# Token sums of the norms over 128 columns, running sums first, and high passes first in the two units behind them

## The reference

```python
def rms_norm(x, g):
    y = xf * lax.rsqrt(jnp.mean(xf * xf, axis=-1, keepdims=True) + RMS_EPS)
    return (y * g.astype(jnp.float32)).astype(x.dtype)
...
def layer_norm(x, g, b):
    mu = jnp.mean(xf, axis=-1, keepdims=True)
    var = jnp.mean(jnp.square(xf - mu), axis=-1, keepdims=True)
    y = (xf - mu) * lax.rsqrt(var + LN_EPS)
    return (y * g.astype(jnp.float32) + b.astype(jnp.float32)).astype(x.dtype)
...
    x = layer_norm(ALPHA * x + mix, ln1_g, ln1_b)
    up = causal_dwconv_2(jnp.einsum('bsd,df->bsf', x, w_up), ffn_conv_w)
    ffn = jnp.einsum('bsf,fd->bsd', jax.nn.silu(a) * b, w_down)
    return layer_norm(ALPHA * x + ffn, ln2_g, ln2_b)
```

## Time and profile before

| | us |
|---|---|
| median of 3 runs | 1235.99 |
| lowest and highest | 1234.67, 1236.5 |
| the profiled execution | 1236.2 |
| its span, first to last instruction | 1234.4 |
| PE busy | 1208.5 (98%) |
| DVE busy | 844.7 (68%) |
| ACT busy | 705.9 (57%) |
| POOL busy | 399.6 (32%) |
| mean granted clock of PE | 0.992 |

### The profile page before, as it was taken

How to read it: one execution, slowest core, us unless ns; L and a number is a source line. 1 busy time by engine, 2 the same in 40 slices (tenths; PEclk the granted TensorE clock), 3 DMA queues, 4 the chain that set the end, 5 groups by cost and what they waited for, 6 DMA issues and landing times. The chain is left out here.

```text
span 1234.4 us, 27264 instructions
## 1 busy us (share of the span) xinstructions
PE 1208.5 (98%) x10242; PEld 1183.6 (96%) x10242; DVE 844.7 (68%) x1458; ACT 705.9 (57%) x1228; POOL 399.6 (32%) x376
## 2 busy tenths in 40 slices
PE   8999999999999999999999999999999999999997
PEld 8998989999999999999999999999999999999997
DVE  5867664676777765767677777755766677777655
ACT  4666566545666654466455666644466555666642
POOL 2006214023334402210338434314610339343313
PEclk8999999999999999999999999999999999999999
DMA  6554445665566666454653666565554654566662
GB/s 242 187 166 142 137 133 153 194 191 169 172 188 197 189 192 189 154 158 151 188 174 123 186 187 198 173 205 155 154 171 142 187 180 128 186 190 187 199 190 87
DMA packets 60288, 212.70 MB, mean 172 GB/s; under 512 B 6688, under 2 KB 7968, under 8 KB 60064
## 3 DMA queue, kind: packets, MB, share of 16 engines
q1 hardware_dynamic: 60192, 211.39, 55.8%
HBM read 210.31 MB, written 1.05 MB: 171 GB/s over the span
## 5 line engine op out<-in xcount | busy, mean ns | idle before, releaser
L1391 DVE TENSOR_TENSOR wlo<-raw,whi 128x1024 fp32r<-128x1024 f32 (+1 forms) x400 | 489.5, 1225 | 302.0 <-ACT whi L733 300.0
L1065 PE MATMUL bank<-shifted,whi 128*128 128x256 f32 x2296 | 639.3, 278 | 1.3 <-POOL shifted L667 1.1
L1066 PE MATMUL bank<-shifted,whi 128*128 128x256 f32 x2296 | 636.2, 277 | 0.0
L1067 PE MATMUL bank<-shifted,wlo 128*128 128x256 f32 x2296 | 635.9, 277 | 0.0
L733 ACT ACTIVATE whi<-raw 128x1024 fp32r<-128x1024 f32 (+1 forms) x400 | 415.7, 1040 | 146.7 <-PE bank L1067 134.4
L1065 PEld LDWEIGHTS bank<-shifted,whi 128*128 128x128 f32 x2296 | 431.5, 188 | 3.1 <-POOL shifted L667 1.3
L1067 PEld LDWEIGHTS bank<-shifted,wlo 128*128 128x128 f32 x2296 | 431.7, 188 | 0.0
L1066 PEld LDWEIGHTS bank<-shifted,whi 128*128 128x128 f32 x2296 | 431.1, 188 | 0.0
L634 POOL TENSOR_TENSOR fprod<-ugate,uval 128x256 f32<-128x256 f32 x66 | 99.4, 1506 | 210.1 <-DVE uval L1736 204.5
L1065 PE MATMUL bank<-fhi,whi 128*128 128x256 f32 x528 | 146.1, 277 | 0.0
L1067 PE MATMUL bank<-fhi,wlo 128*128 128x256 f32 x528 | 145.8, 276 | 0.0
(11 more groups left out here) (212 smaller groups left out, 1276.4 us busy)
## 6 DMA issues: line engine op xcount, KB each, us to landing
raw<-in_w_win SPq DMA_DIRECT2D x140, 512.0 KB, 3.6
raw<-in_w_up SPq DMA_DIRECT2D x132, 512.0 KB, 3.6
raw<-in_w_down SPq DMA_DIRECT2D x48, 448.0 KB, 3.8
raw<-in_w_merge SPq DMA_DIRECT2D x32, 512.0 KB, 3.9
raw<-in_w_out SPq DMA_DIRECT2D x24, 512.0 KB, 3.6
raw<-in_w_down SPq DMA_DIRECT2D x24, 512.0 KB, 3.6
x<-in_x SPq DMA_DIRECT2D x4, 256.0 KB, 4.6
rgw<-in_rg_w SPq DMA_DIRECT2D x1, 1024.0 KB, 9.8
```

The lines of the kernel that those rows point to most:

```text
L1065: pe.matmul(ps, whi[:, slot, w], hi, start=first, stop=False)
L1066: pe.matmul(ps, whi[:, slot, w], lo, start=False, stop=False)
L1067: return pe.matmul(ps, wlo[:, slot, w], hi, start=False, stop=last)
L1391: dve.tensor_tensor(wlo[:, n % RING, w], raw[:, n % RING, w], whi[:, n % RING, w].bitcast(f32), ALU.subtract) \
```

## The change

- PSUM is one tensor of which the banks are slices. A token sum moves 128 columns of ones in place of one, so every column of the result is the same sum; the two halves of the tokens go to two banks, and DVE and ACT read one column of each with a stride.
- PE sums what POOL has added first, then does one or two warm products, and then sums the last tile. In mix 26 warm products stand ahead in place of 18, and the running sum comes last. In a layer norm the four warm products ahead of the sums are gone, and three stand in place of none ahead of the spread of the mean, one in place of three behind it.
- DVE makes the deviation of a tile right behind its residual (in wout from tile 4 on), and in a layer norm the diagonal of the mean behind the variance.
- ACT squares one tile earlier in the down stages, and in wout at other units; it makes the high part of one more weight unit ahead of the last square of a layer norm, which in before came behind the root (in mix that of unit 0 ahead of the root).
- In a ramp PE does the two products with `xhi` for tile k of both units as soon as `xhi` is there, and then the product with `xlo` of tile k - 1. The very first ramp keeps the old order within a tile.

```diff
@@ -288,12 +288,14 @@
 
-        bank = [ctx.enter_context(nc.psum_tensor(f"bank{i}", [P, 512], f32)) for i in range(8)]
+        psum = ctx.enter_context(nc.psum_tensor("psum", [P, 8 * 512], f32))
+        bank = [psum[:, 512 * i:512 * (i + 1)] for i in range(8)]
...
 
-        square_sums, dev_sums, shift_sum = ps_misc[:, 0:2], ps_score[:, 0:2], ps_stat[:, 0:S]
-        spread_inverse, spread_mean = ps_out[:, 0:S], ps_turn[:, 0:S]
+        square_banks, dev_banks, shift_sum = (ps_out, ps_misc), (ps_score, ps_turn), ps_stat[:, 0:S]
+        square_sums, dev_sums = psum[:, 5 * 512:7 * 512 + 1:2 * 512], psum[:, 3 * 512:4 * 512 + 1:512]
+        spread_inverse, spread_mean = ps_turn[:, 0:S], ps_stat[:, S:2 * S]
@@ -684,7 +686,7 @@
 
-                    ring = 2 if which[:3] == "ln2" and t < 4 else 4
+                    ring = 2 if which[:3] == "ln2" and t < 5 else 4
@@ -780,8 +782,8 @@
                 act.activation(dev[:, t, :], x[:, t, :], ACT.Square).then_inc(squared, 1)
+            hi_part(0)
             norm_root("mix", RMS_EPS)
-            hi_part(0)
@@ -952,7 +954,7 @@
                 elif t >= 4:
-                    act.wait_ge(added_q, ACCQ[which] + t - 2)
+                    act.wait_ge(added_q, ACCQ[which] + (max(1, t - 4) if which[:3] == "ln1" else 3))
@@ -963,11 +965,13 @@
                     if which in LNI:
-                        due = {3: [0], 4: [1, 2], 5: [3], 6: [4], 7: [5, 6]}.get(t, [])
+                        due = {4: [0, 1], 5: [2, 3, 4]}.get(t, [t - 1] if t > 5 else [])
...
                         square(which, u)
+                if which in LNI:
+                    hi_part(first + KT + 2)
@@ -975,15 +979,18 @@
 
-                    if i % 3 == 1 and not (isinstance(it, int) and i < 6):
-                        square(which, i // 3 - 2, it)
+                    if i % 3 == 1 and not (isinstance(it, int) and i < (6 if which in LNI else 3)):
+                        square(which, i // 3 - 1, it)
+                    if which in LNI and i == 5 and isinstance(it, int):
+                        square(which, 0)
...
                 repeat(act, name, DOWN, 6, body, peel_first=True)
-                square(which, KT - 2)
+                if which in LNI:
+                    hi_part(START[name] + DOWN + 2)
@@ -1047,13 +1054,10 @@
                 norm_root(f"ln1{l}", LN_EPS)
-                hi_part(START[f"up2{l}"] + 2)
...
                 norm_root(f"ln2{l}", LN_EPS)
-                if l < LAYERS2 - 1:
-                    hi_part(START[f"win2{l + 1}"] + 2)
@@ -1083,22 +1087,42 @@
 
-            TOGETHER = [(u, k) for k in range(KT) for u in range(2)]
-            LATER = [(u, k) for u in range(2) for k in range(5)] + TOGETHER[10:]
-            def ramp(n, result, ready, order=TOGETHER, split=(xhi, xlo)):
-                hi, lo = split
+            LATER = [(u, k) for u in range(2) for k in range(5)] + [(u, k) for k in range(5, KT) for u in range(2)]
+            def first_ramp(ready):
                 met = [0, 0]
-                for u, k in order:
+                for u, k in LATER:
                     if k == 0:
-                        begin(n + u, result + u)
+                        begin(u, u)
...
                     met[u] = k + 1
-                    mm = product_of(bank_of(result + u)[:, 0:S], (n + u) % RING, k, hi[k], lo[k], k == 0, k == KT - 1)
+                    mm = product_of(bank_of(u)[:, 0:S], u, k, xhi[k], xlo[k], k == 0, k == KT - 1)
...
                         mm.then_inc(unit_done, 1)
+            def ramp(n, result, high, low, split=(xhi, xlo)):
+                def with_low(k):
+                    pe.wait_ge(*low[k])
+                    for u in range(2):
+                        mm = pe.matmul(bank_of(result + u)[:, 0:S], whi[:, (n + u) % RING, k * P:(k + 1) * P], split[1][k], start=False,
+                                       stop=k == KT - 1, skip_group_check=True)
+                        if k == KT - 1:
+                            mm.then_inc(unit_done, 1)
+                for k in range(KT):
+                    pe.wait_ge(*high[k])
+                    for u in range(2):
+                        if k == 0:
+                            begin(n + u, result + u)
+                        for part in (whi, wlo):
+                            pe.matmul(bank_of(result + u)[:, 0:S], part[:, (n + u) % RING, k * P:(k + 1) * P], split[0][k],
+                                      start=k == 0 and part is whi, stop=False, skip_group_check=True)
+                    if k:
+                        with_low(k - 1)
+                with_low(KT - 1)
@@ -1109,18 +1133,19 @@
 
+            def highs(which):
+                return [(x_hi, XHI[which] + t + 1) for t in range(KT)]
...
 
-            def token_sums(dst, sources):
+            def token_sums(banks, src, ready, count, first=False, last=False):
+                pe.wait_ge(ready, count)
                 for h in range(2):
-                    for i, (src, ready, count) in enumerate(sources):
-                        if h == 0:
-                            pe.wait_ge(ready, count)
-                        mm = pe.matmul(dst[:, h:h + 1], src[:, h * P:(h + 1) * P], ones[:, 0:1], start=(i == 0),
-                                       stop=(i == len(sources) - 1))
+                    mm = pe.matmul(banks[h][:, 0:P], src[:, h * P:(h + 1) * P], ones[:], start=first, stop=last)
@@ -1129,9 +1154,9 @@
                 released(result)
+                token_sums(square_banks, acc[:, 0, :], added_q, ACCQ[which] + KT - 2, first=True)
                 warm(2, result)
-                sources = [(acc[:, 0, :], added_q, ACCQ[which] + KT - 2), (dev[:, KT - 1, :], squared, SQ[which] + KT)]
-                token_sums(square_sums, sources).then_inc(summed, 1)
+                token_sums(square_banks, dev[:, KT - 1, :], squared, SQ[which] + KT, last=True).then_inc(summed, 1)
@@ -1139,10 +1164,10 @@
 
-                warm(18, 0)
-                mm = token_sums(square_sums, [(acc[:, 0, :], added_q, FIRST_SUMMED - 1), (dev[:, KT - 2, :], squared, KT // 2),
-                                              (dev[:, KT - 1, :], dve_squared, KT // 2)])
-                mm.then_inc(summed, 1)
+                warm(26, 0)
+                token_sums(square_banks, dev[:, KT - 2, :], squared, KT // 2, first=True)
+                token_sums(square_banks, dev[:, KT - 1, :], dve_squared, KT // 2)
+                token_sums(square_banks, acc[:, 0, :], added_q, FIRST_SUMMED - 1, last=True).then_inc(summed, 1)
@@ -1156,14 +1181,15 @@
                 released(result)
-                warm(4, result)
-                token_sums(dev_sums, [(acc[:, 1, :], added_d, (KT - 2) * (i + 1)), (dev[:, KT - 1, :], centred, KT * (i + 1))]) \
-                    .then_inc(dev_summed, 1)
-                token_sums(square_sums, [(acc[:, 0, :], added_q, ACCQ[which] + KT - 2), (tmp[:, 3, :], dev_squared, KT * (i + 1))]) \
-                    .then_inc(summed, 1)
+                token_sums(dev_banks, acc[:, 1, :], added_d, (KT - 2) * (i + 1), first=True)
+                token_sums(square_banks, acc[:, 0, :], added_q, ACCQ[which] + KT - 2, first=True)
+                warm(1, result)
+                token_sums(dev_banks, dev[:, KT - 1, :], centred, KT * (i + 1), last=True).then_inc(dev_summed, 1)
+                token_sums(square_banks, tmp[:, 3, :], dev_squared, KT * (i + 1), last=True).then_inc(summed, 1)
+                warm(3, result)
...
                 spread_out(spread_mean, 0).then_inc(mean_spread, 1)
-                warm(3, result)
+                warm(1, result)
@@ -1304,7 +1330,7 @@
                 split = split_of(base)
-                ramp(START[name], RESULT[name], [(m_lo, base + k + 1) for k in range(KT)], split=split)
+                ramp(START[name], RESULT[name], [(m_hi, base + k + 1) for k in range(KT)], [(m_lo, base + k + 1) for k in range(KT)], split)
@@ -1316,7 +1342,7 @@
-                            ramp(n, r, lows(which))
+                            ramp(n, r, highs(which), lows(which))
@@ -1340,7 +1366,7 @@
-            ramp(0, 0, lows("mix"), LATER)
+            first_ramp(lows("mix"))
@@ -1356,7 +1382,8 @@
-                ramp(START[name], RESULT[name], lows("ln20" if l else "final"))
+                norm = "ln20" if l else "final"
+                ramp(START[name], RESULT[name], highs(norm), lows(norm))
@@ -1441,11 +1468,11 @@
                 link(dve.tensor_scalar(statistic(NMEAN), dev_sums, -1.0 / DM, None, ALU.mult))
-                on_diagonal(0, NMEAN, mean_ready)
...
                 dve.scalar_tensor_tensor(statistic(VAR), square_sums, 1.0 / DM, statistic(MEAN2), ALU.mult, ALU.subtract).then_inc(var_ready, 1)
+                on_diagonal(0, NMEAN, mean_ready)
@@ -1717,11 +1744,11 @@
                     if which in LNI:
-                        for u in {3: [0, 1], 4: [2, 3]}.get(t, [t - 1] if t > 4 else []):
+                        for u in {3: [0, 1], 4: [2, 3]}.get(t, []):
...
```

(14 more changed lines are left out.)

## The result

| | before | after |
|---|---|---|
| median of the runs, us (20 each, same chip) | 1235.46 | 1239.27 |
| lowest and highest | 1234.01, 1237.78 | 1235.71, 1242.35 |
| ratio of the medians, 95% interval | | 1.0031 (1.0024 to 1.0038) |
| the profiled execution, its span | 1236.2, 1234.4 | 1239.97, 1238.2 |
| mean granted clock of PE | 0.992 | 0.996 |

The change makes the kernel 3.8 us slower. The forecast was 1232.5 us with a range of 1228.6 to 1235.8; both the sign and the range are wrong. The mean granted clock went up, so the loss is not simply "more time at half clock": over its 20 runs after has 0.996 in the mean, and before has 0.994 over the 80 runs that were taken beside the experiments.

What follows compares the result with a forecast made beforehand. TensorE, busy 98%, was taken as the bound, so only its stretches without weight products or at half clock could move the end. Terms summed to 3.5 us gained: 1236.2 to 1232.7, 1232.5 as median, range 1228.6 to 1235.8.

Steps and rivals of the forecast that it cites:

- ln10 and ln11 up to the first scaling, +0.2 and -0.65: Norms behind wout: GpSimd's last addition sets the sums' start; ln10 gains 0.2 us, ln11 loses 0.65, ramp terms included.
- With 0.33 for GpSimd's later start: In ln10, GpSimd starts on the mean later, priced at 0.33 us; ln11 was said to have that delay already.
- Clock, -0.8: In ln10 and ln11, PE idle without warm matmuls lets the clock fall in one of two: 0.8 us lost.
- Mix, +1.35: In mix, more warm matmuls fill PE's hole, so root and first scaling come earlier: 1.35 us gained.
- ln20, +2.0: Norm behind a down stage: earlier variance and mean diagonal parallel to the root bring first scaling forward, net 2.0 us gained.
- final, +0.35, ffn, +0.1, ln21, +0.25: Final saves a sum, 0.35 us; ffn's ramp starts earlier, 0.1; ln21's earlier variance gains 0.25.
- wout20 and wout21, +0.66: Ramps of wout20 and wout21: high passes first shorten PE's work behind the last low part, 0.33 us each, 0.66 together.
- Column width, 0: Token sums with 128 columns of ones keep the pace of one column: 0 us, bounds -0.03 and +0.03 each.
- rival D: 92 passes of wide token sums take 0.03 us more each, 2.8 us in all: 1235.3 us, chance 0.04.
- A: GpSimd not late in wout; variance of ln10 and ln11 as early as ln20's: 1228.7 us, chance 0.17.
- B: Clock falls in ln10, ln11 and ln20, or mix's first unit data come late: about 1234.9 us, chance 0.19.
- C: PE enters the ramps at half clock, 8.5 us lost at the five inner norms: 1240.2 us, chance 0.06.

Runs made afterwards that it cites:

- spread copy: GpSimd's copy of recentred tiles cut into three pieces behind its first three products of up; ratio to before 1.0001 in after, 0.9968 in before.

## Why the prediction was wrong, point by point

- **ln10 and ln11 up to the first scaling, +0.2 and -0.65: the size.** The rule was right: GpSimd's last addition sets PE's start, and PE stands idle ahead of it. The sizes were off. The last addition ends 2.98 and 3.29 us behind the last pass, where the forecast's 661.35 is 2.6 behind it (658.73 in before); the idle time is 2.17 and 2.47 us instead of 1.85. The forecast's first scalings lie 6.7 and 6.8 us behind the last pass (665.4 less 658.73, 1034.5 less 1027.74). After has 7.27 and 7.75 without a dip in the norm and 8.96 and 8.73 with one: a mean of 8.2 against before's 6.2, so 1.9 us a layer are lost here. The spread copy doesn't bring this part back, the order and squares of before do.
- **The missing term: what GpSimd does behind the norm.** The step "With 0.33 for GpSimd's later start" priced the later mean up to the third scaling and stopped there. What is queued on GpSimd behind the recentring, the copy and then the first product of up, has no term in the sum. PE's idle time at unit 5 (E) rose from 1.1 to 2.2 us. 0.9 of it go when the mean is first again, and the runs give 3.1 us for that step with the copy in one piece and 1.1, within the noise, with the copy spread.
- **Both together.** From the Sum column, before's mean is 193.8 and after's 196.9 us, 3.1 us lost a layer, 6.1 in all, against the forecast's 0.45 and 0.8 for the clock. Undone one at a time, the order gives 1.5 a layer in the traces (its dips with it), the squares 0.9, the mean 1.0; then the Sum is 193.4, a little under before's value. The ratios of whole runs say it with other weights: 1.0033, 1.0031, 1.0014, 0.9989. That the order is a large share stands in the traces only.
- **Clock, -0.8.** One dip was taken, in a norm. Both traces of after have two around the norms behind wout, one in a norm and one over the products behind unit 5 of up2, a place the forecast didn't look at since the late chain led there. The price in a norm was too small as well: 1.2 and 1.5 us more in A against 0.85. What the forecast also left out is that before's three traces all have a dip in ln20 and after's two none; over all runs after spends less time at half clock than before (0.996 against 0.994).
- **Mix, +1.35.** The step up to the first scaling was right in size: a mean of 12.63 in eleven traces of changed kernels against 13.94 in three of before, 1.3. Most of it is given back: in seven of the eleven the clock falls at 18 to 22 us, over dense products of the first units, and unit 2 starts at 23.43 in the mean against 23.80. What stays is 0.4. Window of after's second trace: 

```profile
19.00:20.00 1.00, 1.00 (x6) 0.50 0.78 299
```

- **ln20, +2.0.** Variance 2.60 us behind the last pass, forecast 2.5: right. (The 5.66 us for seven tiles that the step cites from rows 8 stand in the earlier trace rows.) From last pass to unit 2 after takes 13.3 us and before 14.9, 14.4 and 14.3 in three traces: 1.0 to 1.6 gained. The rest of the 2.0 is the +0.25 at the ramp and, against the two later traces, a dip of before that cost less there. Unit 2 stands 8.42 behind the first scaling where before had 8.13 to 8.32, so what the ramp gives (0.25 against the old one) the later mean takes.
- **final, +0.35, ffn, +0.1, ln21, +0.25.** In final 0.25 to 0.4 is gained from last pass to unit 2, as forecast. In ffn nothing: 11.30 us in after against 11.23. In ln21 0.1 from last pass to the end. All three are small.
- **wout20 and wout21, +0.66.** The ramp of wout20 itself gains 0.2 to 0.3 in after, but win2 and wout together, from unit 2 to the last pass, are 0.5 us longer in the first layer (159.9 in the mean of eleven traces against 159.4 of three) and 0.1 in the second. The gain is not there; where in win2 it goes wasn't followed.
- **Column width, 0.** Right: 0.113 us a pass at 128 columns, so rival D has nothing to show. By the Trainium skill's section "Back-to-back issue gap" of "TensorE: Matmul & The Clock Gate" narrow matmuls follow each other faster than ones of 128 columns. These f32 sums don't agree: two passes of one column take 0.24 us, two of 128 columns 0.23.
- **The rivals.** A fell, GpSimd is late. B has the right sign of correction with too few places. C named the slower side and put it in the ramps at half clock; at the ramps there is no dip in after's two traces. The slower side came by a norm that was later than taken and by a wait that the list didn't hold.

The account of the whole: 6.1 lost in two layers, against 0.4 in mix, 0.3 at final, 1.2 at ln20 and 0.1 at ln21 gained, 0.6 lost in win2 and wout, and 0.2 in the stage up to wout1 (276.1 against 275.9 in traces), which makes 4.9. The medians have 3.8 to 4.2. With the three parts undone the same sum is a gain of 2.0, measured 1.4.

## What to carry to other kernels

A late step can cost twice, and the two must be told apart: once by what waits for it at once (here the first scaling), and once by what is queued behind it on its own engine. For the second, read that engine's list on from there until the first instruction that somebody else waits for, even if it lies two stages on; an engine that is busy a third of the time can hold 16 us of work between a norm and its next deadline. A few bulk instructions without a deadline (here a copy) belong behind the first ones that have one: that alone was worth 4 us to the kernel before. But a remedy that helps does not show that it removes the cause: it has to be tried on the kernel before as well, and here it helped both alike. And a gain read from one trace of a noisy stage (mix: 14.85, 13.81, 13.16) wants a second trace.

## What the runs showed of the hardware

- A dense stage of passes can run at 113.3 or at 117.8 ns a pass at granted clock 1.00, for the whole of down1 and only there, 1.7 us; the same program shows both.
- Warm products over one idle place left the time as it was (1.0027 and 1.0049, after 1.0031 and 1.0034) and the mean granted clock over all runs too (0.996 and 0.995, after 0.996 and 0.995). In the traces the dips stand at the place that isn't covered (687 us; A 8.86 and 8.55). With the idle time itself gone, as with the spread copy, up2 has no dip in four of four traces; the kernels with the copy in one piece have one in five of ten.
- The additions of GpSimd that meet a low part of VectorE take 1.7 instead of 0.72 us, as the earlier trace rows had it, in the kernels before and after and with old order or squares alike. Behind the last such addition come two short ones with the old squares and three without them (old order, ln11), and that one short addition is the whole of the 0.7 us between B's 2.4 and 3.1.
